# The adaLN modulation of a two-layer transformer trunk: part of its vector-matrix products moved from TensorE to VectorE, its gate rows spread through DRAM

## The reference, cut to what matters

```python
ms = jnp.split(jax.nn.silu(c) @ ada_w[l] + ada_b[l], 6, axis=-1)
mc = jnp.split(jax.nn.silu(c_ctx) @ ada_w[l] + ada_b[l], 6, axis=-1)
h_lat = modulate(rmsnorm(x_lat, pre_mix_g[l]), ms[0], ms[1])
...
x_lat = x_lat + ms[2] * rmsnorm(o_lat, post_mix_g[l])
f_lat = modulate(rmsnorm(x_lat, pre_ffn_g[l]), ms[3], ms[4])
...
x_lat = x_lat + ms[5] * rmsnorm(y_lat, post_ffn_g[l])
```

## Time and profile before

| | |
|---|---|
| median of 3 runs | 1927.09 us (1927.06 to 1927.76) |
| the profiled execution | 1922.89 us, its span 1921.0 us |
| TensorE / VectorE / ScalarE busy | 1768.6 / 1331.0 / 1099.1 us |
| start, to the first projection matmul | 0 to 59 us |
| projection, layer 0 | 59 to 130 us |
| attention loop, layer 0 | 130 to 275 us |
| output projection and norms, layer 0 | 275 to 339 us |
| FFN, layer 0 | 339 to 690 us |
| norms, projection, layer 1 | 690 to 785 us |
| attention loop, layer 1 | 785 to 863 us |
| output projection, norms, routing | 863 to 940 us |
| experts | 940 to 1900 us |

### The profile page before, as it was taken

One profiled execution on the slowest core, in us unless ns is written; L12 is line 12 of the kernel. 1 busy time (PEld: TensorE's weight loads), 2 busy tenths in 40 slices (PEclk: granted clock), 3 DMA queues, 4 the chain that ended last, 5 costly groups with the idle time before them and its releaser, 6 DMA issues.

```text
span 1921.0 us, 24495 instructions
## 1 busy us (share of the span) xinstructions
PE 1768.6 (92%) x8208; PEld 1412.8 (74%) x8208; DVE 1331.0 (69%) x1595; ACT 1099.1 (57%) x1408; POOL 26.6 (1%) x45
## 2 busy tenths in 40 slices
PE   5899988999999979978599999999999999999993
PEld 1775567788888857646488888888888888888883
DVE  1445765443333455474599999999999999999994
ACT  2333434322222244344487888878888888888883
POOL 2000000000000000000000000000000000000000
PEclk7899999999999989997799999999999999999997
DMA  9438762534443323564599999999999999999992
GB/s 310 154 121 278 254 208 88 182 125 162 134 132 99 95 59 99 175 208 154 196 394 371 376 388 359 395 368 381 383 362 394 366 381 389 360 394 363 382 384 91
DMA packets 232655, 504.91 MB, mean 263 GB/s; under 512 B 15672, under 2 KB 38352, under 8 KB 232320
## 3 DMA queue, kind: packets, MB, share of 16 engines
q1 hardware_dynamic: 229312, 493.49, 71.3%
q0 software_dynamic: 3264, 10.39, 1.9%
HBM read 496.48 MB, written 19.92 MB: 269 GB/s over the span
## 4 chain that ended last, share of the span: by engine, by line
issue 52%; PE 37%; DVE 6%; DMA 2%; ACT 2%; POOL 0%; SPq 0%; POOLq 0%; ACTq 0%; DVEq 0%
PE ps L493 11%; PE ps L495 10%; PE ps L494 10%; PE ps L519 2%; DMA raw<-in_ada_w 1%; DVE w_lo L1196 1%; DMA pg_bc<-in_post_ffn_g 1%; PE ps L641 1%; PE ps L669 1%; PE ps L534 1%; PE ps L543 1%; DVE xs L1309 1%; DVE hT_lo L1283 0%; DVE gg L1243 0%; DVE gg L1242 0%
## 5 line engine op out<-in xcount | busy, mean ns | idle before, releaser
L1196 DVE TENSOR_TENSOR w_lo<-raw,w_hi 128x1024 fp32r<-128x1024 f32 x570 | 685.2, 1223 | 298.6 <-ACT w_hi L897 264.2
L1109 ACT ACTIVATE w_hi<-raw 128x1024 fp32r<-128x1024 f32 x448 | 473.8, 1061 | 106.7 <-PE ps L495 106.7
L493 PE MATMUL ps<-w_hi,he_hi 128*128 128x512 f32 x896 | 354.6, 396 | 0.7 <-DVE he_lo L1528 0.7
L495 PE MATMUL ps<-w_hi,he_lo 128*128 128x512 f32 x896 | 350.4, 391 | 0.0
L494 PE MATMUL ps<-w_lo,he_hi 128*128 128x512 f32 x896 | 349.8, 390 | 0.0
L1196 DVE TENSOR_TENSOR w_lo<-raw_more,w_hi 128x1024 fp32r<-128x1024 f32 x224 | 273.9, 1225 | 45.7 <-ACT w_hi L1109 26.3
L1109 ACT ACTIVATE w_hi<-raw_more 128x1024 fp32r<-128x1024 f32 x224 | 237.8, 1063 | 53.5 <-PE ps L495 53.5
L897 ACT ACTIVATE w_hi<-raw 128x1024 fp32r<-128x1024 f32 x122 | 128.7, 1063 | 214.3 <-PE ps L495 214.3
L495 PEld LDWEIGHTS ps<-w_hi,he_lo 128*128 128x128 f32 x896 | 168.8, 188 | 36.1
L493 PEld LDWEIGHTS ps<-w_hi,he_hi 128*128 128x128 f32 x896 | 169.0, 189 | 34.9 <-issue 1.0
L494 PEld LDWEIGHTS ps<-w_lo,he_hi 128*128 128x128 f32 x896 | 169.0, 189 | 33.9
(11 more groups left out here) (206 smaller groups left out, 1950.3 us busy)
## 6 DMA issues: line engine op xcount, KB each, us to landing
raw<-in_moe_w SPq DMA_DIRECT2D x448, 512.0 KB, 6.1
raw_more<-in_moe_w SPq DMA_DIRECT2D x224, 512.0 KB, 6.1
raw<-in_ada_w SPq DMA_DIRECT2D x96, 512.0 KB, 6.0
raw<-in_ffn_w SPq DMA_DIRECT2D x66, 512.0 KB, 3.8
raw<-in_w_in SPq DMA_DIRECT2D x40, 512.0 KB, 3.8
raw<-in_w_out SPq DMA_DIRECT2D x16, 512.0 KB, 7.7
yrows<-in_x SPq DMA_DIRECT2D x8, 512.0 KB, 6.8
xe<-xrows SPq DMA_DIRECT2D x8, 512.0 KB, 6.6
```

The costliest lines, as they stand in the source:

```text
L493: pe.matmul(o, lh, rh, start=start, stop=False)
L495: return pe.matmul(o, ll, rh, start=False, stop=stop)
L1109: act.activation(w_hi[:, s % SPL, :], expert_raw(i), ACT.Copy).then_inc(hi_done, 1)
L1196: dve.tensor_tensor(w_lo[:, s_ % SPL, :], src, w_hi[:, s_ % SPL, :].bitcast(F32), ALU.subtract)\
```

## The change

Eight chunks stay on the old path: 0 to 3 at the start, and the four of parts 3 and 4 of layer 0 in steps 4, 7, 10 and 13 of the attention loop. The other eight parts (1024 columns each) come as eight units of 128 rows x 1024 columns. VectorE adds up, per partition, weight times silu(c), for one or two streams, in `acc`; the sum over partitions is four fp32 matmuls with ones, and shifts and scales are turned by four transposes. Part 2 of layer 0 is accumulated in its input projection, five parts (1.0, 1.1, 0.5, 1.3, 1.4 as layer.part) in the FFN, 1.2 in the projection of layer 1 and 1.5 in its attention loop. VectorE, no longer TensorE, gives the slots of these units back. A gate is one row of 1024: VectorE adds the bias and multiplies by the gain on 4 x 32 rows, GpSimd's queue writes four pieces of 2 KB to DRAM and reads them back spread over 128 partitions. GpSimd's first loads wait for all 16 units of the start instead of four; layer-norm parameters of layer 1 are loaded later, into the same tiles. The constants lose 376 columns. `arow` moves into the place of `ws_raw`. Semaphores of the two layers are merged, with counts to match.

```diff
+ADA_SEQ = [(0, p, h) for p in (0, 1, 3, 4) for h in range(2)]
+ADA_AT = {4: 4, 7: 5, 10: 6, 13: 7}
+PARTS = [(0, 2), (1, 0), (1, 1), (0, 5), (1, 3), (1, 4), (1, 2), (1, 5)]
+FFN_SUM = {16: 1, 28: 2, 40: 3, 52: 4, 64: 5}
+FFN_ACC = {**{i: 1 for i in (*range(4, 12), *range(20, 28), *range(32, 40))}, **{i: 2 for i in (*range(44, 48), *range(56, 60))}}
+GATE_STEP = 1
...
+def streams(i):
+
+    return 2 if PARTS[i] in ((0, 2), (0, 5), (1, 0), (1, 1)) else 1
...
+        for jn, j in enumerate(IN_ORDER[:4]):
+            for u in range(4):
+                project(j, u, u + 1)
+                acc(1 if 3 <= 4 * jn + u < 11 else 0)
...
+            acc(1 if l and t >= 2 else 0)
+            step_end[l, t] = len(units)
...
@@ sync
+                    if o.split:
+                        sp.wait_ge(lo_done, o.s + 1)
+                    elif o.acc:
+                        sp.wait_ge(sg("acc"), acc_count(o))
+                    else:
+                        sp.wait_ge(ada_used, o.a + 1)
...
@@ gpsimd
+            def gate_rows(n):
+                l, part = PARTS[GATES[n]]
+                pool.wait_ge(sg("gate row"), n + 1)
+                for q in range(4):
+                    pool.dma_start(grows[n, q:q + 1, :], gate_row[n][32 * q:32 * q + 1, :]).then_inc(sg("gate out"), 16)
+                pool.wait_ge(sg("gate out"), 64 * (n + 1))
+                if n == 2:
+                    pool.wait_ge(sg("z pm0"), 2 * NB)
+                for r in range(streams(GATES[n])):
+                    for half in range(2):
+                        pool.dma_start(gg[:, gate_at(l, part // 3, r), 512 * half:512 * half + 512],
+                                       grows[n, 2 * half + r, :].partition_broadcast(P)).then_inc(sg("gates in"), 16)
+
+            pool.wait_ge(ada_used, 16)
...
+            layer_norm_params(0)
+            pool.wait_ge(sg("ada fin"), 4)
+            spatial_params(0)
+            gate_params(0)
+            gate_rows(0)
+            gate_params(1)
...
@@ tensor
+            def acc_sum(i, bank):
+
+                pe.wait_ge(sg("acc"), acc_end[i])
+                for half in range(2):
+                    for r in range(2):
+                        q = 2 * half + r
+                        m = pe.matmul(ps[32 * q:32 * q + 32, bank, :], ones[:, 0:32],
+                                      acc[:, min(r, streams(i) - 1), 512 * half:512 * half + 512], start=True, stop=True,
+                                      tile_position=(0, 32 * q))
+                m.then_inc(sg("acc sum"), 1)
...
+                    if t == GATE_STEP:
+                        acc_sum(GATES[2 * l], ADA)
...
+                if l:
+                    acc_sum(GATES[3], ADA)
                 us = at["out", l, 1]
...
+                        if 12 * g + 2 * (c - c0) in FFN_SUM:
+                            pe.wait_ge(sg("y sum"), NB * 2 * g)
+                            acc_sum(FFN_SUM[12 * g + 2 * (c - c0)], 4)
...
@@ vector
+                for r in range(n):
+                    if k == 0:
+                        ins = dve.tensor_scalar(acc[:, r, :], raw_at(u.k), cstat[:, k, r:r + 1], None, ALU.mult)
+                    else:
+                        dve.wait_ge(sg("acc"), before + n * (k - 1) + r + 1)
+                        ins = dve.scalar_tensor_tensor(out=acc[:, r, :], in0=raw_at(u.k), scalar=cstat[:, k, r:r + 1], in1=acc[:, r, :],
+                                                       op0=ALU.mult, op1=ALU.add)
+                    ins.then_inc(sg("acc"), 1)
...
+            def part_row(i, bank):
+
+                dve.wait_ge(sg("acc sum"), i + 1)
+                if gate_of_row[0]:
+                    dve.wait_ge(sg("gate out"), 64 * gate_of_row[0])
+                if i in MODS:
+                    dve.tensor_copy(arow[:, :], ps[:, bank, :]).then_inc(sg("arow"), 1)
+                else:
...
+                    link(dve.tensor_tensor(row[:, :], ps[:, bank, :], ab_bc[:, :], ALU.add))
+                    dve.tensor_tensor(row[:, :], row[:, :], pg_bc[:, :], ALU.mult).then_inc(sg("gate row"), 1)
...
             def ada_copy(c, bank):
                 dve.wait_ge(ada_used, 4 * (c + 1))
+                if gate_of_row[0]:
+                    dve.wait_ge(sg("gate out"), 64 * gate_of_row[0])
                 dve.tensor_copy(arow[:, :], ps[:, bank, :]).then_inc(sg("arow"), 1)
...
+                    if t == GATE_STEP + 1:
+                        part_row(GATES[2 * l], ADA)
+                    if t >= 2:
+                        take(step_end[l, t])
```

More of the change, by code:

```diff
@@ L93, in constants, with __init__, add, acc @@
     return c
-def spread(t, c0, c1, steps):
-    c = c0 + -(-t * (c1 - c0) // steps)
-    return c if 0 <= t < steps and -(-(t + 1) * (c1 - c0) // steps) > c - c0 else None
 def ada_slot(l, t):
-    if l == 0:
-        return spread(t, 4, ADA_L1, NB * HEADS)
-    return spread(t, ADA_L1, 24, NLAT * HEADS)
+    return ADA_AT.get(t) if l == 0 else None
+def streams(i):
+    return 2 if PARTS[i] in ((0, 2), (0, 5), (1, 0), (1, 1)) else 1
 class Unit:
-    def __init__(self, k, s, a, src, split, shape):
-        self.k, self.s, self.a, self.src, self.split, self.shape = k, s, a, src, split, shape
-def plan_units(ada_w, w_in, w_out, w1, w3, w2):
-    units, at = [], {}
-    n = dict(s=0, a=0)
-    def add(key, src, split, shape):
-        u = Unit(len(units), n["s"] if split else None, None if split else n["a"], src, split, shape)
-        n["s" if split else "a"] += 1
+    def __init__(self, k, kind, n, src, shape):
+        self.k, self.src, self.shape = k, src, shape
+        self.split, self.acc = kind == "s", kind == "c"
+        self.s = n if kind == "s" else None
+        self.a = n if kind == "a" else None
+        self.c = n if kind == "c" else None
+def plan_units(ada_w, w_in, w_out, w1, w3, w2):
+    units, at, step_end = [], {}, {}
+    n = dict(s=0, a=0, c=0)
+    def add(key, src, split, shape, kind=None):
+        kind = kind or ("s" if split else "a")
+        u = Unit(len(units), kind, n[kind], src, shape)
+        n[kind] += 1
         units.append(u)
         at.setdefault(key, []).append(u)
+    def acc(count):
+        for _ in range(count):
+            i, k = n["c"] // KD, n["c"] % KD
+            l, p = PARTS[i]
+            add(("acc", i), ada_w[l][P * k:P * (k + 1), D * p:D * (p + 1)].rearrange("(k p) n -> p k n", p=P), False, (1, UW), "c")
     def tall(w, k0, nk, c0, nc_):
@@ L163, in plan_units @@
                         add(("w2", g, n2), tall(w2[0], c, 2, 512 * n2, 512), True, (2, 512))
-    return units, at, n["s"]
+                        acc(FFN_ACC.get(i, 0))
+                        i += 1
+    assert n["c"] == KD * len(PARTS)
+    return units, at, n["s"], step_end
 def program(nc, x, c, ctx, c_ctx, ada_w, ada_b, pre_mix_g, post_mix_g, pre_ffn_g, post_ffn_g, w_in, w_out,
@@ L508, in ada_rows @@
                 if c and which[0] == 0:
-                    if two_gates(c - 1):
-                        pe.wait_ge(sg("ada fin"), c)
-                    else:
-                        pe.wait_ge(sg("arow"), c)
+                    pe.wait_ge(sg("arow"), c)
+                if c == 4:
+                    pe.wait_ge(sg("gate row"), 1)
                 for u in [at["ada", c][i] for i in which]:
@@ L1185, in _ @@
             chain = [0]
+            gate_of_row = [0]
             stage_end = [in_end[0]]
@@ L1197, in split_lo, with gather_part @@
                     .then_inc(lo_done, 1)
-            def split_upto(s):
-                s = min(s, stage_end[0])
-                while cur[0] <= s:
-                    u = split_units[cur[0]]
-                    split_lo(u.s, raw_at(u.k), u.s + 1)
-                    cur[0] += 1
+            def gather_part(u):
+                i, k = u.c // KD, u.c % KD
+                before = acc_end[i - 1] if i else 0
+                n = streams(i)
+                dve.wait_ge(raw_in[u.k % RAW], raw_count(u.k))
+                if k == 0 and i:
+                    dve.wait_ge(sg("acc sum"), i)
+                for r in range(n):
[6 more added lines that the diff above has]
+                    ins.then_inc(sg("acc"), 1)
@@ new lines, in take @@
+            def take(k):
+                while cur[0] < k:
+                    u = units[cur[0]]
+                    if u.split:
+                        split_lo(u.s, raw_at(u.k), u.s + 1)
+                    if u.acc:
+                        gather_part(u)
+                    cur[0] += 1
+            def split_upto(s):
+                k = split_units[min(s, stage_end[0])].k + 1
+                while k < len(units) and units[k].acc and not (units[k].c // KD == GATES[3]):
+                    k += 1
+                take(k)
@@ new lines, in part_columns, with col @@
+            def part_columns(i, bank):
+                l, part = PARTS[i]
+                w = part // 3
+                dve.wait_ge(sg("acc T"), MODS.index(i) + 1)
```

(12 more changed lines are left out.)

279 lines of the change are left out of this document (157 added, 122 removed).

## The result

The changed kernel takes **1898.61 us** (median of 4 runs, 1897.90 to 1901.43), the kernel before in the same job 1927.07 (1926.53 to 1927.76): ratio 0.9855, 95% interval 0.9838 to 0.9872. The profiled execution took 1897.9 us, its span 1896.1, against 1922.89 and 1921.0 before: 25.0 us less, where the sum had said 37; the medians differ by 28.5. The forecast of 1890 was 8.6 us too low and the time lies inside the range.

What follows compares the result with a forecast made beforehand. Experts and FFN were taken as TensorE-bound, the start as DMA-bound, attention as partly limited by a VectorE-ScalarE loop. Terms -10 - 31 + 9 - 6 + 1 = -37 gave 1885.9 us profiled, 1890 median; range 1863 to 1908 with two rivals.

Steps and rivals of the forecast that it cites:

- Start: Start of the kernel: software queue's loads wait for all 16 units, so the chain ends earlier, -10 us, bounds 0 and 11.
- The start does not move: Rival for the start: units wait for TensorE at 1.2 GHz, not for bytes; -27 us in all, 1900; chance 0.12.
- Gate trip in layer 0: Layer 0's attention: gate row's DRAM trip takes 5 to 9.6 us with 10.4 between, cost 0; exposed +5 to +10, chance 0.1.
- Attention, layer 0: Layer 0's attention loop: ten of 14 chunks leave, -31 us, bounds 22 and 37.
- 1.9 for a head norm: Layer 0's attention: time of a head norm in VectorE's queue, 1.9 us, used to forecast the steps.
- the clock rival: Attention loop: TensorE's clock falls to 1.2 GHz in half of layer 0's steps, +39 us, 1929; chance 0.03.
- The walk: Attention loops: each step timed by the longer of two paths; layer 0 130.07 to 100 us, layer 1 77.2 to 71.2.
- FFN: FFN: 64 VectorE operations, 7.4 us of sums and turns on TensorE, some 1.5 of stalls; +9, bounds 7 and 16.
- Attention, layer 1: Layer 1's attention loop: six chunks leave, but steps 2 to 9 each get an accumulation; -6 us, bounds +3 and -21.
- PEclk below 0.9 in a loop: Attention loops: named sign of being wrong, TensorE's granted clock under 0.9, where 1.00 is 2.4 GHz.
- VectorE decides: Rival, mainly FFN: late accumulations hold up weight loads; 1989 us if all 96 operations are exposed, 1940 if half; chance 0.08.
- TensorE's count: Rival for both attention loops: counting TensorE alone, layer 0 gives 37 us and layer 1 21; total -58, 1869; chance 0.17.

Runs made afterwards that it cites:

- e1: Kernel before with only GpSimd's first wait moved from 4 units to 16: 1918.09 us, ratio 0.9954.
- e2: Changed kernel with GpSimd's first wait back at 4 units and the first gate's parameters loaded ahead of the shift-and-scale wait: 1909.91 us, ratio 0.9911.
- e7: Changed kernel with 40 filler matmuls into an unused bank where TensorE waited around steps 6 and 9 of layer 0's attention: 1896.93 us, ratio 0.9842.
- e8: Changed kernel with Copy in place of Sqrt in both attention loops' head and spatial norms, so no table loads: 1895.17 us, ratio 0.9815.
- e4: Changed kernel with the second gate's row loads and third gate's parameter loads moved from the FFN's middle to its last group: 1897.47 us, ratio 0.9850.
- e3: Changed kernel with VectorE's 84 multiply-and-add operations left out, unit loads, sums and turns kept: 1891.92 us, ratio 0.9813.
- e10: Changed kernel with the last gate's eight accumulations moved from layer 1's attention into its input projection: 1895.94 us, ratio 0.9835.
- e12: As e11, with the attention loops' square roots taken as Exp of half of Ln in place of Sqrt: 1909.80 us, ratio 0.9917.
- e11: Changed kernel with e4's moved loads and the last gate's accumulations in layer 1's projection, none before its fourth unit: 1891.30 us, ratio 0.9821.

## Why the prediction was right, and where its terms were off

**Start, right.** -11.1 for -10. Two readings agreed in the forecast, the arrival of the unit at the full rate (10 to 11) and the queue's share of the DMA engines' time (9.8), and e1 bears out both: -9.9. Neither is a law of the price: with 1.38 of the 2.23 MB and 8.5 us of share e2 still pays in full. The unit behind which twelve of the third chunk's rows came at 37.67 us now let them go on at 27.53, inside the 27 to 29 of the forecast, and TensorE was granted 1.00 in 25 to 30 us where the earlier trace rows have 0.50. *The start does not move* is refuted.

**Gate trip in layer 0, right at 0.** The row was ready at 137.96 us, the four stores took 2.06 us to issue, they landed 1.6 us after their issue in the median, and the `arow` copy that waits for them came at 148.45:

```profile
138.25 2.06 POOL L503 DMA_DIRECT2D grows<-arow  x4 [89.89 <-DVE arow L1346]
...
141.68 2.17 POOL L509 DMA_DIRECT2D gg<-grows  x4 [1.36 <-DMA grows<-arow]
```

3.7 us used of the 10.5. The later landing that the Trainium skill's box on "DVE blocks DMA" (SBUF — State Buffer) made possible doesn't show here, though VectorE worked without a gap from 137.27 to 141.07 us, the stretch of these four stores. Whether any of its operations there takes both ports, which the box asks for, no run shows.

**Attention, layer 0: mis-sized by 7 us.** The step that failed is "1.9 for a head norm". It was read in a trace in which VectorE arrived at the root late, when the table was loaded already. With the rows gone it arrives on time and waits 1.35 us more, twice, and TensorE behind it falls to 1.2 GHz in steps 7 and 10. That is the mechanism of the clock rival, at a chance of 0.03: it came in two steps of the 16, not in half of them, and cost 1.5 to 3 us in the step where e7 isolates it. By e8, 6.0 us of the 7.0 go with the table loads (4.1 to 6.1 against the other runs). The Trainium skill's section HAM oscillation (TensorE: Matmul & The Clock Gate), cited in the prediction, is borne out in this: idle gaps in a working loop brought the lower clock back, 0.50 at 160 to 165 us behind waits of 1.58 and 0.97, and with the gaps filled it stayed at 1.00 (e7). The walk itself was good: without the table loads steps 6 to 10 are 6.0, 6.1, 5.5, 8.8 and 8.9 for a forecast of 5.5, 6.2, 5.7, 10.4 and 7.1, and eleven of the 15 steps were right within 0.6 us as they ran.

**FFN: +12.1 for +9.** Inside its bounds of 7 and 16. (Its marks of 360 and 367 us, 9 and 16 above the window of 351 us in the earlier trace rows, don't compare with the 376.3: cut at its first and last matmul the FFN is 364.2 before.) By the intervals between its matmuls: four of the five sums 1.09 each (4.4; the fifth lies in the wait of the last block), four turns 0.37 each (1.5), two waits for VectorE's sums 1.6, which makes 7.5 of the 8.9 forecast for these; then 2.7 for the gate loads (e4), about 1.0 in twelve intervals of 0.3, and 0.6 at 1.2 GHz. The 2.7 is a term that the sum didn't have: the DRAM trip was priced in layer 0 and called harmless at the end, and the second gate's loads in the FFN's middle, eight transfers on GpSimd's queue, were not followed to what they meet there.

**Attention, layer 1: -2.0 for -6.** The direction of the walk was right (steps 3 to 5 within 0.6 us), step 6 and the end were not: 31.1 us for 26.2. Two terms were mis-sized. In step 6, 8.3 for 6.5, an accumulation lies beside the head norm's table load: without accumulations it stays at 8.3 (e3, e10), since VectorE then stands 1.35 us for the root in their place, and with them but without the table loads it is 7.7 (e8). Each hides the other; a run without both was not made. The end, 22.8 for 19.7, holds accumulations in its chain, 1.2 us of waiting for each of three, and about 1.5 us of TensorE's clock, which also falls there without them (e1, e3). Without the multiply-and-adds and at the lower clock it is 19.5 (e3), without accumulations and at the higher one 17.4 (e10), and the whole stage then takes 66.7 us. Here a sign of being wrong that the prediction had named came true: PEclk below 0.9 in a loop, 0.86. How the walk split its 19.7 isn't written in it, so which part of the 3.1 us it had left out stays open.

**Output projection, layer 0: +1.7.** Not foreseen; after 2.4 us of waiting at its start TensorE had 0.54 in the window 246 to 249 us. The kernel before has the same wait of 2.4 us. In all profiles of it and its variants, and in e2, e4 and e8, the stage took 63.2 to 63.8 us, in the other variants of the changed kernel 65.5 (e12: 67.0). So it comes in some executions, at the same instructions, and fits the clock; whether the change makes it likelier stays open.

**Projections**, cost 0: right. **VectorE decides**, the rival that ends slower: refuted by e3, with 7.4 of 107 us exposed. **TensorE's count**: refuted too. Layer 0 gave 24.0 of its 37 us and 28.4 without the table loads (e8), layer 1 2.0 of its 21 and 10.5 without the accumulations (e10).

The miss of 12 us, in one line: head norm and clock in layer 0 7, layer 1's attention (head norm, accumulations, clock) 4, FFN 3, output projection 2, and -4 from the start, the projections and the rest. The changed kernel's profile was the fastest of its four runs and lucky in step 1: 5.0 us near the 4.7 of the forecast, where all but one of the other profiles of the changed kernel and its variants have 6.5 or more.

## What to carry to other kernels

A duration read in a trace holds only with the arrival order of that trace: where a change takes away what one engine waited for, look at each wait that ended early behind it (here a table load that ScalarE did meanwhile), and price it as if the waiter came on time. Follow every transfer of a moved step to the window in which it is issued; a few broadcast loads held up a weight unit by 11 us here. And when a change bundles several edits, try the smallest alone: one constant in a wait was 9.9 of the 25 us. Last, hold a stage's gain against the totals of all runs: here one trace each says that the table loads cost 0.8 us before and 6.0 after, and the medians don't say so.

## What the runs showed of the hardware

**The granted clock is not the same from one execution to the next at the same instruction.** After the same wait of 2.9 us in step 0, the changed kernel's profile shows 1.00 and e11's 0.61, and step 1 took 5.0 us in one and 6.5 in the other (windows of 3 us, columns as above):

```profile
127.00:130.00 3.00, 2.95 (x14) 2.24 (x15) 1.99 (x6) 1.29 (x4) 0.00 (x0) 1.00 0.00 0
```
```profile
128.40:131.40 3.00, 2.90 (x9) 2.12 (x10) 1.99 (x6) 1.29 (x5) 0.00 (x0) 0.61 0.00 0
```

Over all profiles of the changed kernel and its variants step 1 took 4.9 to 7.7 us, step 7, where nothing was done about it, 7.6 to 9.1, the start (e2 aside) 47.8 to 51.0, and in the FFN 8 to 23 of 1584 intervals between matmuls were at 1.2 GHz. It isn't the chip alone: e2, e3 and e4 ran on one, and their steps 1 took 6.5, 7.7 and 4.9 us. This may be most of the 3 to 9 us between the runs of one kernel; only profiled executions can be read, so that isn't shown.

**A table load costs its 1.28 us and no more on ScalarE**: the instruction behind it starts 0.01 us after its end (e12's rows).
